# One activation table set for Ln and Exp, and one sigmoid load ahead of the feed-forward loops, in a four-layer mixer network

## What is computed

```
h = rms_norm(x, g) * (1 + scale) + shift      # scale, shift, gate from silu(c) @ ada_w + ada_b
x = x + gate * mixer(h)
h = rms_norm(x, g2) * (1 + scale2) + shift2
x = x + gate2 * feed_forward(h)
```

```
y = x * rsqrt(mean(x*x) + eps) * g
```

## Time and profile before

| what | value |
|---|---|
| device time, median of three runs | 3785.29 us (3784.98 to 3787.14) |
| span of the profiled execution | 3780.0 us |
| TensorE busy | 3443.9 us, 91% |
| VectorE busy | 1943.2 us, 51% |
| ScalarE busy | 1404.0 us, 37% |
| GpSimd busy | 1158.7 us, 31% |

### The profile page before, as it was taken

The page is one execution under the profiler, slowest core; times in us unless marked ns, Lnnn a source line. Parts: engine busy times, 40 slices in busy tenths (PEclk is TensorE's granted clock), DMA queues, the critical chain, the costliest instruction groups (busy, mean ns, idle before and its releaser), DMA issues. The chain is left out here.

```text
span 3780.0 us, 62105 instructions
## 1 busy us (share of the span) xinstructions
PE 3443.9 (91%) x25014; PEld 2632.7 (70%) x25014; DVE 1943.2 (51%) x2407; ACT 1404.0 (37%) x2305; POOL 1158.7 (31%) x626
## 2 busy tenths in 40 slices
PE   6799989999898999789999998788699999989998
PEld 4344467888676777568888886666478877668876
DVE  8245546556345343556555574454356554853344
ACT  3356633122455555422223443333133324143332
POOL 0000013444455555224443322000034443124443
PEclk8899989999899999889999998787799999989999
DMA  6212214444343434315443221000035443113332
GB/s 240 82 65 67 71 48 148 162 161 155 95 127 114 134 109 113 102 63 193 150 162 107 76 59 40 4 4 4 25 116 185 144 156 100 57 56 98 96 94 79
DMA packets 261707, 383.86 MB, mean 102 GB/s; under 512 B 40406, under 2 KB 185466, under 8 KB 250234
## 3 DMA queue, kind: packets, MB, share of 16 engines
q1 hardware_dynamic: 257144, 366.90, 30.1%
q10 hardware_dynamic: 4354, 13.98, 0.9%
HBM read 360.90 MB, written 19.92 MB: 101 GB/s over the span
## 5 line engine op out<-in xcount | busy, mean ns | idle before, releaser
L487 POOL TENSOR_TENSOR w_lo<-w_raw,w_hi 128x1024 fp32r<-128x1024 f32 x302 | 741.1, 2454 | 1872.1 <-ACT w_hi L478 1872.1
L500 PE MATMUL ps<-h_hi,w_hi 128*128 128x512 f32 x2432 | 959.0, 394 | 75.1 <-DVE h_lo L684 40.2
L501 PE MATMUL ps<-h_hi,w_lo 128*128 128x512 f32 x2432 | 954.4, 392 | 0.0
L502 PE MATMUL ps<-h_lo,w_hi 128*128 128x512 f32 x2432 | 953.6, 392 | 0.0
L478 ACT ACTIVATE w_hi<-w_raw 128x1024 fp32r<-128x1024 f32 x302 | 320.3, 1061 | 1097.3 <-PE ps L502 1068.2
L500 PEld LDWEIGHTS ps<-h_hi,w_hi 128*128 128x128 f32 x2432 | 462.1, 190 | 186.2 <-issue 46.0
L501 PEld LDWEIGHTS ps<-h_hi,w_lo 128*128 128x128 f32 x2432 | 462.3, 190 | 96.3
L502 PEld LDWEIGHTS ps<-h_lo,w_hi 128*128 128x128 f32 x2432 | 461.6, 190 | 96.5
L792 DVE TENSOR_TENSOR h_lo<-big,h_hi 128x512 fp32r<-128x512 f32 x100 | 243.5, 2435 | 228.2 <-ACT h_hi L478 228.1
L1521 POOL TENSOR_TENSOR w_lo<-w_raw,w_hi 128x512 fp32r<-128x512 f32 x192 | 249.1, 1307 | 262.7 <-ACT w_hi L1702 258.4
L615 DVE SCALAR_TENSOR_TENSOR big<-yT,cond,big 128x2048 f32<-128x2048 f32 x63 | 183.2, 2907 | 92.0 <-DMA yT<-in_ada_w 91.7
(11 more groups left out here) (444 smaller groups left out, 5595.2 us busy)
## 6 DMA issues: line engine op xcount, KB each, us to landing
w_raw<-in_mlp_w SPq DMA_DIRECT2D x128, 512.0 KB, 3.6
yT<-in_ada_w SPq DMA_DIRECT2D x56, 1024.0 KB, 5.8
w_raw<-in_dil_w_in SPq DMA_DIRECT2D x192, 256.0 KB, 3.0
w_raw<-in_ffn_w_up SPq DMA_DIRECT2D x176, 256.0 KB, 3.0
h_free<-in_ada_w SPq DMA_DIRECT2D x24, 1024.0 KB, 5.0
w_raw<-in_ffn_w_down SPq DMA_DIRECT2D x44, 512.0 KB, 3.5
w_raw<-in_ab_w_in SPq DMA_DIRECT2D x70, 256.0 KB, 2.8
yT<-in_ada_w SPq DMA_DIRECT2D x32, 512.0 KB, 6.0
```

The lines of the kernel that those rows point to most:

```text
L487: self.nc.gpsimd.tensor_tensor(self.w_lo[:, s, :], self.w_raw[:, s, :], self.w_hi[:, s, :].bitcast(F32), ALU.subtract).then_inc(sg["w_spli ...
L500: self.nc.tensor.matmul(out, w_hi, h_hi, start=start, stop=False)
L501: self.nc.tensor.matmul(out, w_lo, h_hi, start=False, stop=False)
L502: return self.nc.tensor.matmul(out, w_hi, h_lo, start=False, stop=stop)
```

## The change

Everywhere that `natural_log` was named, outside the dilated attention, the set that holds both functions is named, and the loads of the exponential set are taken out. In the heads loop the load is moved out, ahead of the loop. In `conv_ffn` the sigmoid set is loaded ahead of the loop. In RWKV the joint set is loaded once in each turn that had a load of `natural_log` or exp: at the place of the first in odd turns, at that of the second in even ones.

```diff
@@ norm_after
-            nc.scalar.preload_act_table_set(LN)
+            nc.scalar.preload_act_table_set(LN_EXP)
             act.wait_ge(sg["sums"], sg.at("sums", 1))
@@ conv_ffn
+            nc.scalar.preload_act_table_set(SIGMOID)
             rounds(0, range(2, UNITS))
@@ recurrent (HGRN), each period, and the same at its end
-                nc.scalar.preload_act_table_set(LN)
+                nc.scalar.preload_act_table_set(LN_EXP)
...
-                nc.scalar.preload_act_table_set(EXP)
@@ rwkv, each turn
                     if d == 1 and more or ends:
-                        nc.scalar.preload_act_table_set(LN)
+                        nc.scalar.preload_act_table_set(LN_EXP)
...
                     if more or ends:
-                        nc.scalar.preload_act_table_set(EXP)
+                        if not (d == 1 and more or ends):
+                            nc.scalar.preload_act_table_set(LN_EXP)
                         act.drain()
```

## The result

The changed kernel took 3742.56 us (median of four runs, 3738.38 to 3744.33); in the same rounds the kernel before took 3786.22 (four runs). The ratio is 0.9882, with a 95% interval of 0.9868 to 0.9896: faster by 44.7 us, between 39.4 and 50.0. The forecast was 3754.2, with 3743 as its low end.

A forecast was written before the change was run, and what follows sets the result against it. Bound: engines on the path waiting behind table loads. Terms 6.4 + 2.6 + 13.0 + 1.3 + 7.8 = 31.1 us off the 3780.0 us span, plus 5.3 around it: 3754.2 us, range 3743 to 3765.

The forecast's parts named there:

- The heads: Heads' stage: 1.3 us ahead of the loop, 0.65 in each of fourteen heads (9.1), 2.6 in head 14; sum 13.0.
- D: Mainly heads and RWKV: stalls end earlier, clock falls less often, 10 us or more on top; chance 0.08.
- Norms: Waits shortened: 6.4 us over five norms, 2.6 in latent attention ahead of its loop, 1.3 in Fourier's layer norm.
- RWKV: Shorter waits for key roots and the last root, plus turn 7's copies: 0.8, 3.8, 1.9 and 1.3, sum 7.8 us.
- Turn 7: RWKV's turn 7 had two loads and none may be left: nothing to 2.6 us, taken as 1.9.
- Tanh: RWKV's tanh and sigmoid: a possible extra load is covered by a weight load's transfer wait; nothing, bound 1.3 us.
- Feed-forwards and HGRN: Loads there are hidden behind TensorE's products: nothing; feed-forwards 2.6 us lost to 1.8 won, HGRN at most 1.
- Rival A: Whole kernel: a switch costs more than its row, whole-load terms double, some 20 us more, 3734 us; chance 0.03.
- B: Heads' and feed-forward loops keep loads, the set not carried across the loop head; 9 us back, 3763 us; chance 0.07.
- C: Heads: something unseen takes the place of the wait at L1153, the 9.1 us are not gained, 3763 us; chance 0.10.
- E: Product stages that follow: shorter pauses, clock falls more often, kernel ends slower (7.6 us needs a 38.7 us cost); chance 0.02.

The follow-up runs named there:

- e5_one_load: The changed kernel with one load of the joint set put back in each head; 3743.91 us, ratio 0.9896 to the kernel before.
- e2_norms: The kernel before with only the eight norms, latent attention ahead of its loop and the Fourier layer norm on the joint set; 3778.85 us, ratio 0.998.

## Why the prediction came out wrong

The sign and the places were right, and the other terms held within what was measured. What failed is the step "The heads", with its sum 1.3 + 9.1 + 2.6 = 13.0 us. It priced a removed hold-up of TensorE at the time for which TensorE stood still. That count was right: 0.51 us a head where I took 0.65, 2.7 us in head 14 where I took 2.6. But the hold-ups were also paid in clock, for which the term had nothing: behind a few of them TensorE's clock fell, and the products of the loop took 10.7 us more, those of the tail 2.6 us more. In the loop five executions with the hold-up and seven without agree on this; the tail, which took 16.8 to 22.9 us even with the loop at 1.00, moves too much for its 2.6 us to be called shown. By spans the heads gave 23.5 us (20.0, 2.6, and 0.9 ahead of the loop, from the first L1127 to the first score: 10.41 us, now 9.47), by times 24 to 36. The rival that named this, D (10 us or more on top, 3743 us or below), had a chance of 0.08, and 3742.56 us is what it said; of its two places, the heads and RWKV, only the heads show it (RWKV's clock was 0.79 in this pair before and after). The sum of the whole, 31.1 us with nothing for the clock, missed 13.6 of the 44.7 us. I had looked at the mean clock of the whole kernel, 0.933, and not at the clock of the loop, 0.96 with all its loss given back by one edit; that row was there to be read, and would have bounded the gain from above by some 11 us more.

- **Norms** (6.4, 2.6 and 1.3 us): right. 0.07 us between Ln and Exp, 1.35 us for each of the four waits and 1.3 for the fifth, 7.6 us (3 to 12) for 10.3.
- **RWKV** (7.8 us): right within what was measured, 4.9 us (1 to 8) by times, 5.7 us by the stage's means and 1.3 ahead of it. Turn 7 kept its load, since a named load is made though its set is loaded: my 1.9 us there counted on the build to drop it, and that part was wrong.
- **Tanh** (nothing): right, and the load did come, so the build does not count tanh to the joint set. ScalarE after the change:

```profile
2299.21 1.28 ACT L3229 ACT_TABLE_LOAD   x1 [12.87 <-PEq L3526]
...
2301.14 1.28 ACT L3230 ACT_TABLE_LOAD   x1
...
2302.97 0.70 ACT L3185 ACTIVATE tmp<-big,cols 128x512 f32<-128x512 f32 x1
```

  The weight load L2944 behind it waited 7.68 us, for its transfer as before, not for ScalarE:

```profile
2303.75 0.50 PEld L2944 LDWEIGHTS ps<-big,ring 64*128 64x128 f32 x2 [7.68 <-DMA ring<-in_rwkv_g]
```

- **Feed-forwards and HGRN** (nothing): right, 0.8 us slower (5 slower to 3 faster) for nearly 50 us of ScalarE's time.
- **Rival A**: the total fell nearer to its 3734 us than to the forecast, for another reason. The Trainium skill, page "ScalarE: Activation LUTs", section "What ACT_TABLE_LOAD costs", has a drain of about 1380 ns behind a switch; there are 0.07 us where a load went out of a norm that had 1.35, and the one load of e5_one_load that had no cover cost 1.4 us of wait, where the page's sum would make it some 2.66. No run here shows that drain.
- **Rivals B and C**: no load is left in the loops, and the heads gained what stood between copy and projection. **E**: the product stages behind kept their clock (from the end of the heads to RWKV's first score TensorE was busy for 1724.08 us before and 1723.93 after, both at 0.95); the whole mean went from 0.933 to 0.939.

That short stops between groups of products can make the clock go back and forth is also in the Trainium skill, page "TensorE: Matmul & The Clock Gate", section "A second HAM failure mode: psum-queue depth-cycling". Loops at 0.94 to 0.96 with the hold-up and 1.00 without agree with it.

## What to carry to other kernels

Before pricing a wait that goes away on TensorE, read the granted clock of that stretch alone, not of the kernel: where it is below 1.00, count the wait's own length and name the stretch's lost busy time as room above it; at 1.00 the length is all (9.1 us of loop for 8.5 us of idle time here). The room is a bound and no forecast: the heads' loop filled it, and RWKV, at 0.79 before and after, did not. Table loads are worth removing by where TensorE stands behind them: sixteen heads gave most of the gain here, and forty loads beside full products gave none. Every load that was named was made here, so name one only where the set differs, or where the engine waits anyway.

## What was not expected of the hardware

- A hold-up of about half a microsecond in a head of some 17 us, beside one of 0.69 us that alone left the clock at 1.00, decided over the clock of a loop of 250 us: 1.00 in each of the seven executions without it, 0.94 to 0.96 in each of the five with it, whether table loads (four) or further activations (one) made it. The clock did not fall behind each hold-up, but in three to five places of 3 to 7 us among fourteen heads. What in TensorE's activity tips it isn't shown by these runs.
- Of two executions with the same RWKV stage, one was 7.9 us longer than the other (384.53 us in the kernel before, 392.45 in e2_norms), with TensorE's clock at 0.79 and 0.77. A stage far from full TensorE use moves by as much as a change of this kind is worth there, and only several executions tell.
